# Attention's value products with the operands exchanged: values loaded, turned probabilities streamed, outputs turned back

## What is computed

```python
logits = jnp.einsum('nbqhd,nbkhd->nbhqk', qb, kc) + bias
logits = jnp.where(mask[None, :, None], logits, -jnp.inf)
m = jnp.max(logits, axis=-1, keepdims=True)
p = jnp.exp(logits - m)
den = jnp.sum(p, axis=-1)
o = jnp.einsum('nbhqk,nbkhd->nbqhd', p, vc) / jnp.transpose(den, (0, 1, 3, 2))[..., None]
```

## Time and profile before

| | us |
|---|---|
| median of 3 runs | 4728.1 (4726.03 to 4729.05) |
| the profiled execution | 4722.32 |
| its span | 4720.7 |
| attention, first score product to last copy of outputs | 1321.4 to 1703.4 |
| TensorE busy over the span | 4550.3 (96%) |
| VectorE busy | 3161.5 (67%) |
| ScalarE busy | 2181.6 (46%) |

### The profile page before, as it was taken

One profiled execution on the slowest core, in us unless ns is written; L12 is line 12 of the kernel. 1 busy time (PEld: TensorE's weight loads), 2 busy tenths in 40 slices (PEclk: granted clock), 3 DMA queues, 4 the chain that ended last, 5 costly groups with the idle time before them and its releaser, 6 DMA issues.

```text
span 4720.7 us, 76711 instructions
## 1 busy us (share of the span) xinstructions
PE 4550.3 (96%) x25756; PEld 3984.6 (84%) x25756; DVE 3161.5 (67%) x6216; ACT 2181.6 (46%) x3608; POOL 923.1 (20%) x911
## 2 busy tenths in 40 slices
PE   8999999999899989996999999999999999999998
PEld 6777787777789978785999999999988888999997
DVE  6668676674656678455555565666667777778887
ACT  4454444343256752232333343444445555556665
POOL 2332101444112001122011111111112111111111
PEclk9999999999999999998999999999999999999999
DMA  6887766555644445443455456565657657777777
GB/s 214 283 310 266 229 200 204 165 188 176 209 165 147 140 162 187 163 146 124 164 187 190 167 187 204 172 213 192 210 200 238 215 206 245 246 249 268 271 270 255
DMA packets 339406, 971.18 MB, mean 206 GB/s; under 512 B 42089, under 2 KB 75668, under 8 KB 301909
## 3 DMA queue, kind: packets, MB, share of 16 engines
q1 hardware_dynamic: 273784, 804.16, 48.3%
q0 software_dynamic: 28304, 88.03, 8.0%
q10 hardware_dynamic: 37085, 76.04, 4.5%
HBM read 772.82 MB, written 200.58 MB: 206 GB/s over the span
## 4 chain that ended last, share of the span: by engine, by line
PE 51%; DVE 1%; ACT 0%; issue 0%; DVEq 0%; POOL 0%; DMA 0%; ACTq 0%; SPq 0%; POOLq 0%
PE ex_d L2834 14%; PE ex_g L2801 11%; PE ex_g L2803 9%; PE ex_g L2797 7%; PE ex_d L2797 4%; PE ex_d L2828 3%; PE ex_d L2803 2%; PE ex_g L2778 1%; PE ex_d L2778 0%; DVE ex_x L2996 0%; PE ex_d L2809 0%; DVEq L2605 0%; ACT ex_wgh L2881 0%; ACT ex_x L2894 0%; DVE ex_y L3070 0%
## 5 line engine op out<-in xcount | busy, mean ns | idle before, releaser
L2803 PE MATMUL ex_g<-ex_x,ex_wgl 128*128 128x256 f32 (+12 forms) x3456 | 981.7, 284 | 0.0
L2801 PE MATMUL ex_g<-ex_x,ex_wgh 128*128 128x288 f32 (+5 forms) x3584 | 757.1, 303 | 2.4 <-DVE ex_x L2996 2.4
L2803 PEld LDWEIGHTS ex_g<-ex_x,ex_wgl 128*128 128x128 f32 x3456 | 653.6, 189 | 3.9
L2881 ACT ACTIVATE ex_wgh<-ex_wg 128x2048 fp32r<-128x2048 f32 x274 | 523.9, 1912 | 283.0 <-PE ex_g L2803 275.6
L2978 DVE TENSOR_TENSOR ex_wgl<-ex_wg,ex_wgh 128x2048 fp32r<-128x2048 f32 x274 | 626.7, 2287 | 41.3 <-ACT ex_wgh L2881 41.3
L2801 PEld LDWEIGHTS ex_g<-ex_x,ex_wgh 128*128 128x128 f32 x3584 | 593.8, 188 | 11.6 <-DVE ex_x L2996 2.8
L2797 PE MATMUL ex_g<-ex_x,ex_wgh 128*128 128x512 f32 (+6 forms) x1664 | 529.6, 377 | 1.0 <-DVE ex_t L3008 1.0
L699 PE MATMUL prj_p<-prj_wh,prj_ah 128*128 128x512 f32 x1136 | 453.1, 399 | 28.4 <-DVE prj_wl L902 22.8
L2746 POOL DMA_INDIRECT out<-ex_y,ex_cur x82 | 155.4, 1896 | 1509.4 <-ACT ex_y L2902 1241.7
L699 PE MATMUL prj_p<-prj_wh,prj_al 128*128 128x512 f32 x1136 | 446.1, 393 | 0.0
L699 PE MATMUL prj_p<-prj_wl,prj_ah 128*128 128x512 f32 x1136 | 445.9, 393 | 0.0
(11 more groups left out here) (453 smaller groups left out, 9483.2 us busy)
## 6 DMA issues: line engine op xcount, KB each, us to landing
ex_wg<-in_w_gu SPq DMA_DIRECT2D x276, 1024.0 KB, 5.1
ex_wd<-in_w_down SPq DMA_DIRECT2D x276, 512.0 KB, 6.2
qkv_d<-prj_o ACTq DMA_DIRECT2D x144, 256.0 KB, 2.6
sp_rows<-sums_d SPq DMA_DIRECT2D x125, 256.0 KB, 3.1
wo_spare<-qkv_d SPq DMA_DIRECT2D x40, 768.0 KB, 4.2
sp_rows<-in_w_in SPq DMA_DIRECT2D x113, 256.0 KB, 3.1
sp_early<-in_w_in SPq DMA_DIRECT2D x56, 512.0 KB, 5.5
sums_d<-sp_early SPq DMA_DIRECT2D x28, 1024.0 KB, 5.3
```

What stands on the lines that cost most here:

```text
L2801: pe.matmul(out[:, 0:size], h[:, k, j, :], x[:, k, 0:size], start=(k == 0 and x is xh), stop=False)
L2803: last = pe.matmul(out[:, 0:size], l[:, k, j, :], xh[:, k, 0:size], start=False, stop=(k == KD - 1))
L2881: act.activation(flat(wgh[f % 2][:, :, :, :]), flat(wg[f % RAW][:, :, :, :]), ACT.Copy).then_inc(wgh_ready, 1)
```

## The change

`values` exchanges its operands: 64 columns of values are loaded, and the turned probabilities (128 columns) are streamed. The result of a unit comes out turned, head e on partitions 64e to 64e+63, 128 columns (queries), in a bank `obT[u % 2]`. The two heads now alternate inside the loop over key blocks. VectorE copies that bank to `oT` (`save_ot`, new, one 128x128 copy per unit). TensorE turns it back with one 128x128 transpose per unit into a single bank `ob` (`turn_o`, new), and ScalarE copies it to `ao` once per unit (128x128) and no longer once per block (128x512). For the banks, scores have two and no longer three: `scores(u)` waits for the bias step of unit u-2.

```diff
-        sb = [t_.ps(f"s{z}", (P, 2, 2 * P)) for z in range(3)]
+        sb = [t_.ps(f"s{z}", (P, 2, 2 * P)) for z in range(2)]
-        ob = [t_.ps(f"o{z}") for z in range(2)]
+        ob, obT = t_.ps("o", (P, P)), [t_.ps(f"v{z}", (P, P)) for z in range(2)]
...
-                    sp.wait_ge(o_saved, n + 1)
+                    sp.wait_ge(o_saved, PB * (n + 1))
...
-                    if u >= 3:
-                        pe.wait_ge(s_read, 2 * (u - 3) + 2)
+                    if u >= 2:
+                        pe.wait_ge(s_read, 2 * (u - 2) + 2)
...
-                    if j == 0 and n >= 2:
-                        pe.wait_ge(o_saved, n - 1)
-                    for e in range(2):
-                        cols = slice((2 * j + e) * DH, (2 * j + e + 1) * DH)
-                        for k in range(k0, 2):
-                            last = pe.matmul(ob[n % 2][:, cols], ppT[u % 3][:, e, k * P:(k + 1) * P],
-                                             blk[(n - 1 + k) % NB][:, 2, cols], start=(k == k0), stop=(k == 1))
+                    if u >= 2:
+                        pe.wait_ge(ot_ready, u - 1)
+                    for k in range(k0, 2):
+                        for e in range(2):
+                            cols = slice((2 * j + e) * DH, (2 * j + e + 1) * DH)
+                            last = pe.matmul(obT[u % 2][DH * e:DH * (e + 1), :], blk[(n - 1 + k) % NB][:, 2, cols],
+                                             ppT[u % 3][:, e, k * P:(k + 1) * P], start=(k == k0), stop=(k == 1),
+                                             skip_group_check=True)
                     last.then_inc(pv_mm, 1)
+
+                def turn_o(u):
+                    pe.wait_ge(ot_ready, u + 1)
+                    if u:
+                        pe.wait_ge(o_saved, u)
+                    pe.transpose(ob[:, :], oT[u % 2][:, :], ident[:, :]).then_inc(o_mm, 1)
...
-                for step in range(NU + 3):
+                for step in range(NU + 5):
...
-                    if 0 <= step - 3:
+                    if 0 <= step - 5:
+                        turn_o(step - 5)
+                    if 0 <= step - 3 < NU:
                         values(step - 3)
...
-                def save_o(n):
-                    act.wait_ge(pv_mm, PB * (n + 1))
-                    act.activation(ao[n % AO][:, :, 0:DH], ob[n % 2][:, :].rearrange("p (h d) -> p h d", h=HG),
+                def save_o(u):
+                    n, j = divmod(u, PB)
+                    act.wait_ge(o_mm, u + 1)
+                    act.activation(ao[n % AO][:, 2 * j:2 * j + 2, 0:DH], ob[:, :].rearrange("p (h d) -> p h d", h=2),
                                    ACT.Copy).then_inc(o_saved, 1)
...
-                    if j == 3 and n:
-                        save_o(n - 1)
-                save_o(NBL - 1)
+                    if u >= 4:
+                        save_o(u - 4)
...
+                def save_ot(u):
+                    dve.wait_ge(pv_mm, u + 1)
+                    if u >= 2:
+                        dve.wait_ge(o_mm, u - 1)
+                    dve.tensor_copy(oT[u % 2][:, :], obT[u % 2][:, :]).then_inc(ot_ready, 1)
...
+                    if step >= 4:
+                        save_ot(step - 4)
+                    if 2 <= step < NU + 2:
                         save_p(step - 2)
```

More of the change, by code:

```diff
@@ L1584, in attention @@
         (y0_in, gain_ready, high, low, zeros, q_turned, q_ready, k_turned, k_ready, k_kept, s_mm, s_read, p_ready, t_mm, pt_ready, pv_mm,
[L1585 to L1586 removed]
+         ot_ready, o_mm, o_saved) = t_.sems("y0_in gain_ready high low zeros q_turned q_ready k_turned k_ready k_kept s_mm s_read p_ready t_mm "
+                            "pt_ready pv_mm ot_ready o_mm o_saved")
         def first(n):
@@ L1675, in scores @@
                             pe.wait_ge(k_kept, kept[n])
-                    if u >= 3:
-                        pe.wait_ge(s_read, 2 * (u - 3) + 2)
+                    if u >= 2:
+                        pe.wait_ge(s_read, 2 * (u - 2) + 2)
                     for e in range(2):
-                        last = pe.matmul(sb[u % 3][:, e, off:], qz[n % 2][:, 2 * j + e, :], kT[n % 2][:, j, off:],
+                        last = pe.matmul(sb[u % 2][:, e, off:], qz[n % 2][:, 2 * j + e, :], kT[n % 2][:, j, off:],
                                          start=True, stop=True)
@@ L1712, in _ @@
                         scores(step)
-                    if n + 1 < NBL:
+                    if step < NU and n + 1 < NBL:
                         if j == 0:
@@ L1742, in probabilities @@
                                        scale=-1.0, accum_out=ao[n % AO][:, h, DH + 1:DH + 2]).then_inc(p_ready, 1)
-                def save_o(n):
-                    act.wait_ge(pv_mm, PB * (n + 1))
-                    act.activation(ao[n % AO][:, :, 0:DH], ob[n % 2][:, :].rearrange("p (h d) -> p h d", h=HG),
+                def save_o(u):
+                    n, j = divmod(u, PB)
+                    act.wait_ge(o_mm, u + 1)
+                    act.activation(ao[n % AO][:, 2 * j:2 * j + 2, 0:DH], ob[:, :].rearrange("p (h d) -> p h d", h=2),
                                    ACT.Copy).then_inc(o_saved, 1)
                 save_q(0)
-                for u in range(NU):
+                for u in range(NU + 4):
                     n, j = divmod(u, PB)
-                    probabilities(u)
-                    if j == 0 and n + 1 < NBL:
-                        save_q(n + 1)
-                    if j == 3 and n:
-                        save_o(n - 1)
-                save_o(NBL - 1)
+                    if u < NU:
+                        probabilities(u)
+                        if j == 0 and n + 1 < NBL:
+                            save_q(n + 1)
+                    if u >= 4:
+                        save_o(u - 4)
             @block.vector
@@ L1792, in save_p @@
                     dve.tensor_copy(ppT[u % 3][:, :, off:], tb[u % 2][:, :, off:]).then_inc(pt_ready, 1)
+                def save_ot(u):
[3 more added lines that the diff above has]
+                    dve.tensor_copy(oT[u % 2][:, :], obT[u % 2][:, :]).then_inc(ot_ready, 1)
                 save_k(0)
-                for step in range(NU + 2):
+                for step in range(NU + 4):
                     n, j = divmod(step, PB)
@@ L1798, in _ @@
                         add_bias(step)
-                    if j == 2 and n + 1 < NBL:
+                    if step < NU and j == 2 and n + 1 < NBL:
                         save_k(n + 1)
-                    if step >= 2:
+                    if step >= 4:
+                        save_ot(step - 4)
+                    if 2 <= step < NU + 2:
                         save_p(step - 2)
```

3 lines of the change are left out of this document (2 added, 1 removed).

## The result

The changed kernel took 4740.3 us (median of 10 runs, 4732.8 to 4744.2), the kernel before on the same chip 4727.3 (10 runs, 4722.6 to 4729.1). The ratio is 1.0026, with a 95% interval of 1.0018 to 1.0034, so 12.3 us more (8.5 to 16). That is slower by some 0.26% (the interval's low end lies just under 0.2%), inside the range and on the forecast's side, but less than half of the size that the sum gave, +30.6. The predicted time, 4758, is 18 us too high.

The account below looks back on a forecast made before the run. TensorE's instruction list was taken to bound the attention stage. Full units +6.5 us, half units +23.5 and stage end +0.6 made +30.6, so 4753 profiled, 4758 as the median; the range was 4724 to 4790.

Parts of the forecast that it names:

- the sum: Attention stage: full units +6.5 us, half units +23.5, stage end +0.6, together +30.6 us, bounds +18 to +46.
- Third bank at 0: Attention scores: having two banks instead of three was priced at 0, the bias step being over in time.
- the sum of the borders: TensorE in attention: going from 128 loaded columns to part of the array and back costs 0.35 us per unit.
- the high bound: Attention units: border price allowed up to 0.40 us instead of 0.35, 10 us more over 192 units; total bound +46.
- values now 0.84: Full attention unit: the old eight value records cost 0.84 us, the new values with borders and transpose 0.90, so +0.06.
- now 0.40: Half attention unit: the old four value records cost 0.40 us, the new values with borders and transpose 0.68, so +0.28.
- No price at the borders: Rival, attention: changing loaded width costs nothing; full units save 0.29 us, half ones 0.07, 37 in all, 4691; chance 0.10.
- Half a price: Rival, attention: a border price of 0.15 to 0.23 us keeps the kernel within 0.2%, 4725; chance 0.11.
- Halves not side by side: Rival, attention values: the changed order makes a record cost 0.11 us, +0.50 per unit, +96, 4824; chance 0.04.
- ScalarE the link: Rival, attention: ScalarE's output copy holds back the next exponentials, 0.3 us per half unit, 25 more, 4783; chance 0.09.
- The clock: Rival, attention: TensorE drops to 1.2 GHz; a tenth of the stage there would be some +38 us; chance 0.03.
- What would show it: Attention signs: values to scores 0.6 to 0.7 or 0.4 to 0.45 us, turn_o to values 0.2, half unit 1.65, stage 412.

Follow-up runs that it names:

- e1: The kernel before with only two score banks instead of three and the matching wait; 4726.6 us against 4729.6, ratio 0.9997.
- e3: The changed kernel with both heads' results on partitions 0 to 63 and two VectorE copies per unit; 4789.8 us against 4729.6, ratio 1.0126.
- e4: The changed kernel with the outputs' turn moved between the two key blocks' value products in full units; 4778.8 us against 4729.6, ratio 1.0103.
- e2: The changed kernel with each value product loading both heads' 128 columns and writing all 128 partitions; 4756.5 us against 4729.6, ratio 1.0056.
- e11: The changed kernel with two units' values per run, outputs copied one unit later, queries copied before a block's first exponentials; 4712.3 us against 4729.4, ratio 0.9960.
- e6: The changed kernel with a block's four units of values in one run, outputs turned and copied once per block; 4749.8 us against 4725.9, ratio 1.0046.

## Why the prediction was right, and where it was wrong

**What bounds the kernel: right.** TensorE was full at PEclk 1.00 in both stretches, and its list set the end. VectorE's copy took 284 ns (forecast 286), ScalarE's 278 (300, bound 392); in the last stretch both stay about four fifths busy. Third bank at 0: e1.

**Record and the sum of the borders: right; their parts: not.** 0.0545 us a record (e3: 0.109 without the second half). The borders, from the unrounded records: 0.093 into the run (0.20 from `turn_o` to the values, 0.109 where nothing changes), 0.151 at its end (0.587 - 8 x 0.0545; 0.369 - 4 x 0.0545), 0.102 at the first scores (0.968 - 0.866). That is 0.346; taken was 0.35. But the s5 stage, from which the 0.35 came, splits it otherwise: 0.09 in, 0.21 at the run's end, 0.05 behind. So the high bound, which took the parts over one by one, rested on a split that doesn't hold in attention, and e4's extra trip with a transpose behind it cost 0.30 and not 0.35. Why the two totals agree no run shows; that they do is in part luck.

**The step that failed: "values now 0.84" and "now 0.40".** The term for what the change removes was too small by 0.053 us. Its first step was the reading "a value record thus costs 0.105 us": it costs 0.112. The prediction read the distance from values to scores as the whole price of the values and the scores' 0.92 as the scores' own. In truth 0.053 of these 0.92 belong to the values ahead: e2 has the same scores at 0.87. (By the prediction's own method in s5, a long run less a short one, and the earlier trace rows give (0.84 - 0.40) / 4 = 0.11 at once.) So the old values cost 0.893 in a full unit and 0.447 in a half one, and the sum should have read 0.90 - 0.893 = 0 to 0.01 for a full unit and 0.68 - 0.447 = 0.23 for a half one. It measured 0.00 and, in price alone, 0.225. Over 192 units the error is 10.2 us of the 15.5 that the forecast was too high for the stage (30.6 - 15.1).

The same slip sat in a check that the prediction made and passed over: it compared 256-column products behind a run with "0.92 / 2" and so found 0.08 lost there, where against 0.866 / 2 it is 0.11. The number was to be had from the trace of before, in the rows of three scores and seven values shown under e2.

**The rest.** In half blocks TensorE had small pauses before, part of which the longer units took up: 5.55 us a block are 4 x 1.11 + 2 x 0.44 = 5.32 and 0.23 of pauses; after, 6.32 are 4 x 1.34 + 2 x 0.44 = 6.24 and under 0.1. That is 0.03 a unit, 84 x 0.03 = 2.5 us; no run isolates it. The wait of TensorE named "issue" shrank from 2.6 to 0.9 us; the prediction had allowed 0 to -2.6 and taken 0. Together with the 10.2 that is some 14 of 15.5; the remainder is rounding of the sum's terms and the end of the stage, and no run isolates it.

**The rivals.** No price at the borders: refuted by e2 and e4. Half a price: the price measured 0.346, not 0.15 to 0.23; 4740 lies about as far from this rival's 4725 (by its own sum the even point is 4728) as from 4758, because what the change removes had been priced too low and not because the borders were cheap. Two pages of the Trainium skill bear on this. Its page TensorE: Matmul & The Clock Gate, section Measured speedup vs the span model, has no term for entering a pack, and the runs have one of 0.35 us. Its page TensorEngine Tiling (Array Packing), section Performance Considerations, recommends this exchange; by the runs it depends on the number of records between two borders. Four lose 0.225 us, eight break even (the full unit here, and a half block of 5.54 us in e11 against 5.55), more gain. Halves not side by side: they were (e3). ScalarE the link: not in the changed kernel, where TensorE waited 0.5 us for it, but exactly this took e6's gain. The clock: 1.00 in both stretches; only the stage's first 10 us ran at the lower level (granted clock 0.52 before, 0.50 after), so the change did not touch it.

**What would show it.** 0.6 to 0.7 from values to scores in full units: 0.59, just under it; 0.4 to 0.45 in half ones: 0.37, missed, both because the run's end took 0.15 and not the 0.21 of s5. 0.2 from `turn_o` to values: 0.20. Half unit 1.65 us: 1.34 without a turn of queries or keys and 1.78 to 1.87 with one; the mean over a block, 6.32 / 4 = 1.58, is the comparable number. The stage 412: 401.

## What to carry to other kernels

Price what a change removes by the difference between a long run and a short one, not by one group's distance to the next: part of a group's cost can stand in the first record of the next group. Compare the first record of each group with its fellows before calling a group's time its own. And when a cost is paid per change of shape, count trips before records: gather units into longer runs, and then look at which in-order engine has its copy placed ahead of work that is wanted sooner.

## What the runs showed of the hardware

- A record that loads 128 columns costs 0.112 us whether it streams 64 columns (before: (0.840 - 0.394) / 4) or 128 (e2: (0.893 - 0.447) / 4); a 128x128 transpose costs 0.109. With 64 streamed columns the first interval of a run is 0.053 short and the first of the next group 0.053 long.
- Products on alternate halves of the array cost 0.0545 us a record whether the halves take turns after two records or after four (0.587 and 0.594 for a run of eight with its end), and 0.109 on one half alone.
- A round trip from 128 loaded columns to 64 and back costs 0.346 us where scores follow, in three parts: 0.093, 0.151 and 0.102 (0.101 for the 128-column scores of half units: 0.548 against e2's 0.447). One more trip, around a single transpose, cost 0.30 (e4).
